# Gate rows fetched pair by pair, the first scores of the third attention moved up, the last gated chunk normalized on VectorE, attention roots by log and exp, in a two-block float32 transformer kernel

## The chip, the core and the metric

The kernel runs on one core of one Trainium2 chip. The metric is the device time of one launch in microseconds (us), the median of several runs. All data are float32 in HBM.

## The reference

One sequence of 256 tokens, width 1024, goes through two blocks. All matrices are float32.

```python
# first block
x = x + 0.5 * swiglu(rmsnorm(x, ff1_norm), w_gate, w_up, w_down)        # width 2816
proj = rmsnorm(x, mix_norm) @ w_in                                      # gMLP a, q, k, v, gate logits
y_a = gmlp_spatial_gating(gelu(a_in), ...)
y_b = stick_breaking_attention(q, k, v)                                 # 16 heads of 64
g_a, g_b = split(sigmoid(g_logits + b_gate))
x = x + (g_a * (y_a @ w_branch_a) + g_b * (y_b @ w_branch_b)) @ w_out
x = x + 0.5 * swiglu(rmsnorm(x, ff2_norm), ...)
x = rmsnorm(x, final_norm)
# second block
x = x + moba_attention(rms_norm(x) @ w_qkv) @ w_o[0]    # 256 tokens: one block, causal, ALiBi
x = x + squared_relu_mlp(rms_norm(x), ...)              # width 4096
k, v, c = shared_kv(x)                                  # c: running sum of log_sigmoid(h @ w_f + b_f)
x = x + forgetting_attention(rms_norm(x) @ w_q, k, v, c) @ w_o[1]
#   logit[t, s] = q.k / 8 + c[t] - c[s], causal, softmax
x = x + squared_relu_mlp(rms_norm(x), ...)
return rms_norm(x, final_norm)
```

## The kernel before, in words

**Precision.** A float32 product is made of three passes with operands split into a high part (a cast, on ScalarE) and a low part (the difference, on VectorE): low by high, high by high, high by low (`three`, L1273). The feed-forward up products put two of these side by side (L1356 and L1363).

**The weight pipeline.** Every weight tile is a *unit*. The SP queue sends unit c into one of four raw slots (`send`, L281) once the low part of unit c - 4 has been taken (`room`, L277). ScalarE casts it (`hi`, L571, the activation is L578), VectorE subtracts (`lo`, L857, the subtraction is L863), TensorE waits for the low part (`ready`, L1270) and multiplies (L1276 for everything but the up products). The order in which each engine takes units and its other work is written out by hand; an engine never passes over an instruction that waits. The cores of the loops are the same in each stage: `ffn`, `attention`, `chunks`, `w_o`, each once per engine.

**Feed-forward, gated (ff1, ff2).** Eleven chunks of 256 hidden columns. Per chunk TensorE makes four banks of up products, VectorE adds the two halves of each bank (L912, four reductions), POOL multiplies by the token scale `rbc` (`normalized`, L506, instruction L514, in two parts, the first once two reductions are done), ScalarE takes Silu (L622), VectorE multiplies (L919), ScalarE and VectorE split the product (L631, L932), and TensorE runs the down products of the chunk after the up products of the next one. After the last chunk there is no next one. Between chunks of ff1 POOL issues side loads (`side_load`, L425): two layer norm rows of 512 KB at m = 2 and 3, the gate bias broadcast to all partitions into `gates`, 1 MB for each token half, at m = 4 and 6, and a norm row of 512 KB at m = 8.

**Attention (stick, moba, fox).** Units 0 to 7 of a stage are v, for all heads; then four units per pair of heads, two for q and two for k. While v is computed, ScalarE sums the squares of x (`stat`, L580: table set load at L582, Square L589, Sqrt L592), VectorE takes the reciprocal (`root`, L866), ScalarE loads the table set with exp and log again (L703) and goes on with units 6 and 7. In moba two such roots follow each other: the first scales x by the first block's final norm (`final`, L872, instruction L878), the second is taken of the scaled x. Then q and k of pair 0 are projected (`project`, L1424) and copied out with the token scale by VectorE (L978 for q, L983 for k). The scores are L1452 and L1454. VectorE adds the bias and takes the row maximum (`first_part`, L993 and L995), ScalarE takes exp (L658), VectorE normalizes (`second_part`, L1013), TensorE transposes (`middle`, L1474), ScalarE copies (L681), TensorE multiplies by v (`weighted`, L1487 and L1491). A cycle does the middle of pair p, the scores of p + 1, the projection of p + 2.

**Before that loop** the three stages differed in one place. Stick and moba: project pair 0, scores of pair 0, project pair 1. Fox: project pair 0, project pair 1, wait for the gate sums, scores of pair 0; on VectorE q and k of pair 1 are copied out before `first_part(0)`.

**Fox only.** The log forget gates are summed over tokens on TensorE (`gate_sums`, L1516 to L1524, placed before unit 7). VectorE copies the sums (L1058, L1059) and only then takes units 8 and on. POOL writes the sums to DRAM (L555) and reads them back broadcast to all partitions into `c_all`, 16 heads of 128 KB each, in four transfers of 2, 4, 4 and 6 heads issued one behind the other (L559, grouping at L49). `biases` (L445) makes the bias of a pair of heads from it (L460, L462, L467); it waits for the group that holds the head. Biases of pairs 0 and 1 come first, then POOL copies v for the pair (L480, which waits for the weighted product of two pairs back) and the biases of the next pair.

Of the kernel before, what the change touches and what calls it, by code (L numbers as in the profile page):

```python
# [48 lines left out]
C_GROUPS = ((0, 2), (2, 4), (6, 4), (10, 6))  # L49
# [4 lines left out]
STAT = {"ms_done": 2, "rms_done": 2, "rstd_done": 2}  # L54

# [11 lines left out]
def att_sems(extra):  # L67
# [11 lines left out]
    ("turn_mix", TR(1)), ("stat_mix", STAT), ("stick", att_sems(STICK)),  # L79
# [4 lines left out]
    ("turn_moba", TR(1)), ("stat_final1", {**STAT, "x_done": 2}),  # L84
    ("stat_moba", STAT), ("moba", att_sems(SOFT)),
    ("w_o0", {"units": 8, "x_done": 4}),
    ("turn_mlp0", TR(1)), ("stat_mlp0", STAT), ("mlp0", mlp_sems(N_MLP)),
    ("turn_fox", TR(2)), ("stat_fox", STAT), ("fox", att_sems(SOFT)),
# [52 lines left out]
def two_blocks(nc, x_in, ff1_norm, ff1_w_gate, ff1_w_up, ff1_w_down, mix_norm, w_in, b_gate, gmlp_ln_g,  # L141
# [4 lines left out]
    with ctx:  # L146
# [3 lines left out]
        def sem(name):  # L150
# [89 lines left out]
            "c_ready", "ct_done", "cn_done", "ct_out", "c_in0", "c_in1", "c_in2", "c_in3", "shift_done", "stored")}  # L240
# [164 lines left out]
        def _(pool):  # L405
# [19 lines left out]
            def side_load(m):  # L425
# [14 lines left out]
            def causal(buf, h):  # L440
                v = buf[:, h, 0:512].rearrange("p (b t) -> p b t", b=2)[:, :, 0:P]
                return pool.affine_select(out=v, in_=v, compare_op=ALU.is_gt, fill=0.0, base=0,
                                          pattern=[[0, 2], [1, P]], channel_multiplier=-1)

            def biases(phase, pr):  # L445
# [3 lines left out]
                for h in range(2):  # L449
# [5 lines left out]
                    else:  # L455

                        for g, (first, _) in enumerate(C_GROUPS):
                            if n == first:
                                pool.wait_ge(s[f"c_in{g}"], 16)
# [9 lines left out]
                        ins.then_inc(s["bias_done"], 1)  # L469

# [35 lines left out]
            def normalized(phase, n, between=lambda m: None):  # L506
# [3 lines left out]
                for m in range(n):  # L510
# [53 lines left out]
        def _(act):  # L564
# [15 lines left out]
            def stat(phase, ready=None):  # L580

                act.preload_act_table_set("sqrt_and_others")  # L582
                for tok in range(TOK):
# [3 lines left out]
                    elif tok == 0:  # L587
# [5 lines left out]
                        .then_inc(s["rms_done"], 1)  # L593

# [45 lines left out]
            def attention(phase, soft, turn_b, stats):  # L640
# [56 lines left out]

                hi(b + 4)
# [4 lines left out]
                act.preload_act_table_set("natural_log_exp_and_others")  # L703
# [87 lines left out]
            attention("stick", False, lambda: turned("turn_mix", 1, [(xt_hi, 1)]), lambda: stat("stat_mix"))  # L791
# [25 lines left out]
            def two_stats():  # L817
                stat("stat_final1")

                stat("stat_moba")  # L820
# [10 lines left out]
            attention("fox", True, lambda: turned("turn_fox", 1, fox_sets), lambda: stat("stat_fox"))  # L831
# [24 lines left out]
        def _(dve):  # L856
# [14 lines left out]

            def final(phase):  # L872

                for tok in range(TOK):
# [3 lines left out]
                    dve.scalar_tensor_tensor(x[:, tok, :], x[:, tok, :], rstd_f[:, tok:tok + 1], row_gain[:],  # L878
                                             ALU.mult, ALU.mult).then_inc(s["x_done"], 1)
# [18 lines left out]
            def ffn(phase, n, stats):  # L898
# [3 lines left out]
                def chunk(c, m, before=lambda: None):  # L902
# [4 lines left out]
                    for q in range(4):  # L907
                        if q < 3:
                            dve.wait_ge(s["up_done"], at(phase, "up_done") + 3 * m + q + 1)
                        else:  # L910
# [3 lines left out]
                            .then_inc(s["g_done"], 1)  # L914
                    lo(c + 7)
# [55 lines left out]
            def attention(phase, kind, turn_b, stats):  # L971
# [179 lines left out]
            def first_stats():  # L1151
# [17 lines left out]
                      lambda: root("stat_mix"))  # L1169
# [17 lines left out]
            dve.wait_ge(s["gate_in"], 32)  # L1187
# [496 lines left out]
```

## Time and profile before

| What | Value |
|---|---|
| median of 3 runs | 1290.17 us (1289.05 to 1290.55) |
| the profiled execution, own time | 1290.61 us |
| its span, first to last instruction | 1288.8 us |
| TensorE (PE) busy | 1240.5 us, 96% |
| VectorE (DVE) busy | 821.1 us, 64% |
| ScalarE (ACT) busy | 642.1 us, 50% |
| GpSimd (POOL) busy | 177.3 us, 14% |
| mean granted TensorE clock | 0.989 of full |
| DMA | 221.77 MB, mean 172 GB/s |

PE is TensorE's matmuls, PEld its weight loads. Times in a timeline or a chain are in us from the start of the span. Square brackets behind a row give how long the engine had been idle before it and what ended that. The granted clock is a share of full speed: 1.00 is 2.4 GHz, 0.50 is 1.2 GHz. An execution takes 1.8 us more than its span.

### The profile page before, as it was taken

The numbers are of one execution on the slowest core, as the hardware profiler recorded it, in microseconds if no ns is written. First come the engines' busy times: TensorE is split into PE (matmuls) and PEld (weight loads), VectorE is DVE, ScalarE is ACT, GpSimd is POOL, SyncE is SP. The second block draws the span as 40 slices with busy tenths as digits, with TensorE's granted clock in tenths as the row PEclk, the third lists the DMA queues.
The fourth block names the chain that finished last, engine by engine and source line by source line (L and its number), as shares of the span: only waits on it lengthen the run. The fifth ranks groups of instructions, "written<-read, shape, count | busy, mean of one in ns | idle before, by whom it ended". The sixth has DMA issues, their size and how long they took to land.

```text
span 1288.8 us, 17749 instructions
## 1 busy us (share of the span) xinstructions
PE 1240.5 (96%) x6854; PEld 1057.0 (82%) x6854; DVE 821.1 (64%) x1276; ACT 642.1 (50%) x1016; POOL 177.3 (14%) x229
## 2 busy tenths in 40 slices
PE   6999999999999999999999999999999699999997
PEld 5788887898878878888878878888888587888886
DVE  4666676454676566666666767866663476785753
ACT  5444446565654445444456656544445365654442
POOL 0222220022030002222202310000000451000000
PEclk9999999999999999999999999999998799999999
DMA  6676654444746454656654445765542444576550
GB/s 192 209 235 213 195 190 148 131 115 131 241 148 199 163 164 149 195 191 201 193 170 135 128 151 191 262 197 184 194 130 56 153 133 164 185 255 195 187 176 33
DMA packets 174973, 221.77 MB, mean 172 GB/s; under 512 B 9708, under 2 KB 104536, under 8 KB 174632
## 3 DMA queue, kind: packets, MB, share of 16 engines
q1 hardware_dynamic: 173112, 213.20, 52.1%
q0 software_dynamic: 1472, 6.38, 1.5%
q8 instruction: 54, 0.88, 0.3%
q10 hardware_dynamic: 304, 1.05, 0.2%
q14 instruction: 31, 0.25, 0.1%
HBM read 219.53 MB, written 1.06 MB: 171 GB/s over the span
## 4 chain that ended last, share of the span: by engine, by line
PE 74%; DVE 10%; DMA 6%; ACT 4%; POOL 3%; issue 1%; SPq 1%; ACTq 0%; DVEq 0%; POOLq 0%
PE bank L1276 46%; PE bank L1356 14%; PE bank L1363 7%; DVE w_lo L863 5%; DMA raw<-in_ff_w_up 4%; POOL work L514 3%; ACT w_hi L578 2%; DVE work L912 1%; PE bank L1487 1%; DMA raw<-in_w_kv 1%; PE bank L1299 1%; PE bank L1474 1%; DVE xt L894 1%; ACT xt L604 1%; DVE work L919 1%
## 5 line engine op out<-in xcount | busy, mean ns | idle before, releaser
L863 DVE TENSOR_TENSOR w_lo<-raw,w_hi 128x512 fp32r<-128x512 f32 (+1 forms) x496 | 510.7, 1048 | 249.0 <-ACT w_hi L578 247.0
L578 ACT ACTIVATE w_hi<-raw 128x512 fp32r<-128x512 f32 (+1 forms) x496 | 432.3, 898 | 289.9 <-DMA raw<-in_ff_w_up 91.9
L1356 PE MATMUL bank<-xt,w_hi 128*128 128x512 f32 x1216 | 320.3, 396 | 3.5 <-DVE work L912 2.3
L1356 PEld LDWEIGHTS bank<-xt,w_hi 128*128 128x128 f32 x1216 | 215.4, 190 | 42.9 <-DVE work L912 3.8
L1363 PEld LDWEIGHTS bank<-xt,w_lo 128*128 128x128 f32 x1216 | 171.0, 190 | 15.4
L1363 PE MATMUL bank<-xt,w_lo 128*128 128x256 f32 x1216 | 175.4, 282 | 0.0
L1276 PE MATMUL bank<-w_hi,xt 128*128 128x512 f32 x512 | 161.1, 396 | 3.0 <-DVE w_lo L863 2.1
L1276 PE MATMUL bank<-w_hi,yt_lo 128*128 128x512 f32 x336 | 131.9, 393 | 2.0 <-DVE yt_lo L1018 2.0
L1276 PE MATMUL bank<-w_hi,yt_hi 128*128 128x512 f32 x336 | 130.9, 390 | 0.0
L1276 PE MATMUL bank<-w_lo,yt_hi 128*128 128x512 f32 x336 | 130.9, 390 | 0.0
L1276 PE MATMUL bank<-xt,w_hi 128*128 128x256 f32 x640 | 118.5, 286 | 0.0
L1276 PEld LDWEIGHTS bank<-w_hi,xt 128*128 128x128 f32 x512 | 95.7, 190 | 26.1 <-issue 3.9
L514 POOL TENSOR_TENSOR work<-work,rbc 128x512 f32<-128x512 f32 x44 | 76.7, 1763 | 285.0 <-DVE work L912 285.0
L1276 PEld LDWEIGHTS bank<-xt,w_hi 128*128 128x128 f32 x640 | 101.3, 195 | 0.0
L1276 PE MATMUL bank<-xt,w_lo 128*128 128x256 f32 x320 | 95.1, 297 | 5.6 <-DVE kt L983 5.6
L1276 PE MATMUL bank<-w_lo,xt 128*128 128x512 f32 x256 | 100.5, 393 | 0.0
L912 DVE TENSOR_REDUCE work<-bank 128x256 f32<-128x512 f32 x152 | 94.2, 682 | 0.0
L1276 PE MATMUL bank<-w_hi,ht_lo 128*128 128x512 f32 x224 | 88.2, 394 | 3.8 <-DVE ht_lo L932 3.8
L1276 PE MATMUL bank<-w_hi,ht_hi 128*128 128x512 f32 x224 | 88.0, 393 | 0.0
L1276 PE MATMUL bank<-w_lo,ht_hi 128*128 128x512 f32 x224 | 87.8, 392 | 0.0
L1276 PEld LDWEIGHTS bank<-w_hi,yt_lo 128*128 128x128 f32 x336 | 63.1, 188 | 15.7 <-issue 2.8
L1276 PEld LDWEIGHTS bank<-w_lo,yt_hi 128*128 128x128 f32 x336 | 63.1, 188 | 13.2
(181 smaller groups left out, 1216.3 us busy)
## 6 DMA issues: line engine op xcount, KB each, us to landing
raw<-in_w_up SPq DMA_DIRECT2D x64, 512.0 KB, 4.3
raw<-in_w_down SPq DMA_DIRECT2D x64, 512.0 KB, 4.2
raw<-in_ff_w_gate SPq DMA_DIRECT2D x88, 256.0 KB, 4.3
raw<-in_ff_w_up SPq DMA_DIRECT2D x88, 256.0 KB, 4.9
raw<-in_ff_w_down SPq DMA_DIRECT2D x88, 256.0 KB, 2.7
raw<-in_w_in SPq DMA_DIRECT2D x40, 512.0 KB, 4.6
raw<-in_w_in SPq DMA_DIRECT2D x32, 256.0 KB, 3.0
raw<-in_moba_w_qkv SPq DMA_DIRECT2D x32, 256.0 KB, 2.9
```

The costliest lines, as they stand in the source:

```text
L514: pool.tensor_tensor(work[1][:, part, :].rearrange("p (a b) -> p a b", a=2), work[0][:, part, :].rearrange("p (a b) -> p a b", a=2), by_token,
L578: act.activation(w_hi[:, c % RING, 0:w], raw[:, c % RAW, 0:w], ACT.Copy).then_inc(s["hi_ready"], 1)
L604: act.activation(dst[:, k, :], src, ACT.Copy, scale=scale).then_inc(s["tr_hi"], 1)
L863: dve.tensor_tensor(w_lo[:, c % RING, 0:w], raw[:, c % RAW, 0:w], w_hi[:, c % RING, 0:w].bitcast(F32), ALU.subtract).then_inc(s["lo_ready" ...
L894: dve.scalar_tensor_tensor(low[:, k, :], src, gain[:, 8 * g + k:8 * g + k + 1], high[:, k, :].bitcast(F32), ALU.mult, ALU.subtract)\
L912: dve.tensor_reduce(work[0][:, q // 2, (q % 2) * S:(q % 2 + 1) * S], up_banks(m)[q][:].rearrange("p (a b) -> p b a", a=2), AX_X, ALU.add)\
L919: dve.tensor_tensor(work[2][:, 1, :], work[2][:, 0, :], work[1][:, 1, :], ALU.mult)\
L1276: ins = pe.matmul(dst, p, q, start=first and n == 0, stop=last and n == 2)
L1299: ins = pe.transpose(banks[b][:, o:o + P], src[:, tok, k * P:(k + 1) * P], ident[:])
L1356: ins = pe.matmul(up_banks(m)[q][:], w_h[:, k % 2, q * P:(q + 1) * P], flat(xt[:, k, :, :]), start=k == 0, stop=False, skip_group_check=True)
L1363: ins = pe.matmul(up_banks(m)[q][:, 0:S], w_l[:, k % 2, q * P:(q + 1) * P], xt_hi[:, k, :], start=False, stop=k == KT - 1, skip_group_chec ...
L1474: ins = pe.transpose(t_bank[h][:, o * P:(o + 1) * P], work[1][:, h, o * P:(o + 1) * P], ident[:])
```

## The change

1. **Fox, rows of the gate sums.** The four transfers become eight, one per pair (256 KB). Pairs 0 and 1 are issued where the four were; that of pair p + 2 behind the biases of pair p. A bias waits for its own pair's transfer.
2. **Fox, order.** TensorE and VectorE take the order of the two other attentions: the scores of pair 0 before the projection of pair 1, `first_part(0)` before the copies of pair 1. The wait for `cn_done` on TensorE goes.
3. **ff1 and ff2, last chunk.** VectorE multiplies by the token scale itself, behind the second and the fourth reduction, each time after a wait for its own reduction.
4. **Attention roots.** ScalarE takes both sums of squares, then one Ln and one Exp with scale -0.5 over both token columns; Sqrt, VectorE's reciprocals and the load of the Sqrt table set go, and the set with exp and log is loaded ahead of unit 4's cast instead of ahead of unit 6's.
5. **ff1, gate bias.** Four transfers of 512 KB at m = 4, 5, 6 and 7 instead of two of 1 MB.
6. **branch_a.** VectorE takes unit 7's low part behind the first evacuation instead of ahead of it.

```diff
-C_GROUPS = ((0, 2), (2, 4), (6, 4), (10, 6))
+ROOT = {"ms_done": 2, "rms_done": 1, "rstd_done": 1}
...
-                if m in (4, 6):
-                    tok = m // 2 - 2
-                    pool.dma_start(gates[:, tok, :], b_gate.broadcast_to([P, 2 * D])).then_inc(s["gate_in"], 16)
+                if 4 <= m < 8:
+                    tok, half = divmod(m - 4, 2)
+                    pool.dma_start(gates[:, tok, half * D:(half + 1) * D],
+                                   b_gate[:, half * D:(half + 1) * D].broadcast_to([P, D])).then_inc(s["gate_in"], 16)
...
+            def gate_row(pr):
+                rows = c_dram[2 * pr:2 * pr + 2, :].rearrange("(a h) t -> a h t", a=1)
+                pool.dma_start(c_all[:, 2 * pr:2 * pr + 2, :], rows.broadcast_to([P, 2, S]))\
+                    .then_inc(s[f"c_in{pr % 2}"], 16)
...
-                        for g, (first, _) in enumerate(C_GROUPS):
-                            if n == first:
-                                pool.wait_ge(s[f"c_in{g}"], 16)
+                        if h == 0:
+                            pool.wait_ge(s[f"c_in{pr % 2}"], 16 * (pr // 2 + 1))
...
+                if phase == "fox" and pr + 2 < PAIRS:
+                    gate_row(pr + 2)
...
-                for m in range(n):
+                for m in range(n - 1):
                     between(m)
...
-            for g, (h, n) in enumerate(C_GROUPS):
-                rows = c_dram[h:h + n, :].rearrange("(a h) t -> a h t", a=1)
-                pool.dma_start(c_all[:, h:h + n, :], rows.broadcast_to([P, n, S])).then_inc(s[f"c_in{g}"], 16)
+            gate_row(0)
+            gate_row(1)
             pairs("fox")
...
+            def inverse_root(phase, dst=rstd):
+                act.wait_ge(s["x_done"], at(phase, "x_done"))
+                for tok in range(TOK):
+                    act.activation(work[2][:].rearrange("p a b -> p (a b)"), x[:, tok, :], ACT.Square,
+                                   scale=1.0 / 32.0, accum_out=ms[:, tok:tok + 1]).then_inc(s["ms_done"], 1)
+                    act.wait_ge(s["ms_done"], at(phase, "ms_done") + tok + 1)
+                act.activation(rms[:], ms[:], ACT.Ln, bias=eps[:]).then_inc(s["rms_done"], 1)
+                act.wait_ge(s["rms_done"], at(phase, "rms_done") + 1)
+                act.activation(dst[:], rms[:], ACT.Exp, scale=-0.5).then_inc(s["rstd_done"], 1)
...
+                act.preload_act_table_set("natural_log_exp_and_others")
                 hi(b + 4)
                 turn_b()
                 hi(b + 5)
                 stats()
                 act.wait_ge(s["rstd_done"], at(phase, "rstd_done"))
-                act.preload_act_table_set("natural_log_exp_and_others")
                 hi(b + 6)
...
+                        if gated and m == n - 1 and q % 2:
+                            dve.wait_ge(s["g_done"], at(phase, "g_done") + 4 * m + q + 1)
+                            dve.tensor_tensor(work[1][:, q // 2, :].rearrange("p (a b) -> p a b", a=2),
+                                              work[0][:, q // 2, :].rearrange("p (a b) -> p a b", a=2),
+                                              rbc[:].unsqueeze(1).broadcast_to([P, 2, S]), ALU.mult)\
+                                .then_inc(s["nrm_done"], 1)
                     lo(c + 7)
...
                 k_evac(b + 8, 0, 0)
-                if kind == "fox":
-                    q_evac(b + 12, 0, 1)
-                    k_evac(b + 12, 0, 1)
                 first_part(0)
                 lo(b + 16)
                 second_part(0)
-                if kind != "fox":
-                    q_evac(b + 12, 0, 1)
-                    lo(b + 17)
-                    k_evac(b + 12, 0, 1)
-                else:
-                    lo(b + 17)
+                q_evac(b + 12, 0, 1)
+                lo(b + 17)
+                k_evac(b + 12, 0, 1)
...
-            for u in range(4, 8):
+            for u in (4, 5, 6):
                 lo(b + u)
             evac_a(0, 0, b + 3, 0)
-            for u in (8, 9):
+            for u in (7, 8, 9):
                 lo(b + u)
...
             def two_roots():
                 dve.wait_ge(s["gain_in2"], 16)
-                final("stat_final1")
-                root("stat_moba")
+                dve.wait_ge(s["rstd_done"], at("stat_moba", "rstd_done"))
+                for tok in range(TOK):
+                    scaled(tok)
                 dve.wait_ge(s["rstd_done"], at("moba", "rstd_done"))
                 dve.tensor_tensor(rstd[:], rstd[:], rstd_f[:], ALU.mult).then_inc(s["rprod_done"], 1)
...
                 for n in range(4):
                     project(b + 8, 0, n)
-                if kind == "fox":
-                    pe.wait_ge(s["qt_done"], at(phase, "qt_done") + 1)
-                    for n in range(4):
-                        if n == 2:
-                            pe.wait_ge(s["kt_done"], at(phase, "kt_done") + 1)
-                        project(b + 12, 0, n)
-                    pe.wait_ge(s["cn_done"], 1)
-                    scores(0, 0)
-                else:
-                    scores(0, 0)
-                    for n in range(4):
-                        project(b + 12, 0, n)
+                scores(0, 0)
+                for n in range(4):
+                    project(b + 12, 0, n)
```

`scaled(tok)` is the instruction of L878 by itself. In the stages stick, moba and fox `stat` and `root` are replaced by `inverse_root` and nothing; the feed-forward stages and the last norm keep `stat` and `root`.

## Rows read from the trace of the kernel before

**Rows 1.** Timeline of VectorE, branch_a: start, length, instruction, idle before and releaser.

```profile
439.65 0.69 DVE L1121 TENSOR_TENSOR work<-bank,gates 128x512 f32<-128x512 f32 x1 [4.79 <-PE bank L1276]
```

**Rows 2.** Timeline of TensorE, fox, pair 1's first projection to pair 0's weighted product.

```profile
1001.63 0.29 PE L1276 MATMUL bank<-xq_hi,w_lo 128*128 128x256 f32 x1
...
1010.11 0.58 PE L1276 MATMUL bank<-xt,w_lo 128*128 128x256 f32 x1 [5.58 <-DVE kt L983]
...
1021.55 1.66 PE L1474 MATMUL bank<-ident,work 128*128 128x128 f32 x6 [4.97 <-DVE work L1013]
...
1028.29 0.65 PE L1487 MATMUL bank<-work,vn 128*64 128x256 f32 x4
```

**Rows 3.** Chain that ended last, 955 to 1085: start, length, what.

```profile
996.01 12.33 DMA raw<-in_w_kv
```

**Rows 4.** DMA issues, whole run: tile, queue, count, KB each, median us to landing.

```profile
raw<-in_w_kv SPq DMA_DIRECT2D x16, 256.0 KB, 3.0
gates<-in_b_gate POOLq DMA_DIRECT2D x2, 1024.0 KB, 6.0
...
row_gain<-in_final_norm POOLq DMA_DIRECT2D x2, 512.0 KB, 4.8
...
c_all<-c_dram POOLq DMA_DIRECT2D x1, 768.0 KB, 10.9
...
c_all<-c_dram POOLq DMA_DIRECT2D x1, 256.0 KB, 6.5
```

**Rows 5.** Timeline of POOL, fox: first biases, and v's copy in a cycle.

```profile
1002.30 0.40 POOL L460 TENSOR_TENSOR bias<-cn,c_all 128x128 f32<-128x128 f32 x1 [4.47 <-DMA c_all<-c_dram]
...
1004.04 0.40 POOL L460 TENSOR_TENSOR bias<-cn,c_all 128x128 f32<-128x128 f32 x1
...
1046.10 0.52 POOL L480 COPY vn<-side 128x256 f32<-128x256 f32 x1 [3.62 <-PE bank L1491]
```

**Rows 6.** Windows, fox: length, busy by engine, PE clock, DMA share, GB/s.

```profile
1000.00:1005.00 5.00, 4.53 (x39) 4.33 (x38) 0.19 (x1) 0.63 (x1) 2.56 (x6) 1.00 1.03 364
...
1010.00:1015.00 5.00, 4.89 (x23) 4.89 (x24) 0.39 (x2) 0.00 (x0) 0.67 (x2) 0.50 0.18 52
```

**Rows 7.** Timeline of TensorE, moba: the same stretch, in the order of moba.

```profile
696.65 0.49 PE L1452 MATMUL bank<-kt,qt 64*128 64x128 f32 x4 [0.61 <-DVE kt L983]
...
708.06 0.65 PE L1487 MATMUL bank<-work,vn 128*64 128x256 f32 x4
```

**Rows 8.** Timeline of ScalarE and TensorE, moba, behind the roots.

```profile
680.44 1.28 ACT L703 ACT_TABLE_LOAD   x1 [0.22 <-DVE rstd L870]
...
684.11 0.73 PE L1276 MATMUL bank<-w_hi,xt 128*128 128x512 f32 x2 [1.05 <-DVE w_lo L863]
```

**Rows 9.** Timeline of VectorE, last chunk of ff1.

```profile
194.51 2.48 DVE L912 TENSOR_REDUCE work<-bank 128x256 f32<-128x512 f32 x4
...
198.97 0.69 DVE L919 TENSOR_TENSOR work<-work 128x512 f32<-128x512 f32 x1 [1.26 <-POOL work L514]
```

**Rows 10.** Timeline and chain of TensorE, last down products of ff1 and of ff2.

```profile
202.68 0.47 PE L1276 MATMUL bank<-w_hi,ht_lo 128*128 128x512 f32 x1 [2.46 <-DVE ht_lo L932]
...
202.68 5.96 PE bank L1276 x18
...
658.53 0.47 PE L1276 MATMUL bank<-w_hi,ht_lo 128*128 128x512 f32 x1 [1.32 <-DVE ht_lo L932]
...
658.53 4.36 PE bank L1276 x18
```

**Rows 11.** Windows of ff1, POOL chunk to POOL chunk, around the side loads.

```profile
65.19:81.88 16.69, 16.69 (x90) 14.36 (x89) 11.04 (x15) 7.61 (x10) 4.06 (x3) 1.00 0.69 221
...
115.26:133.65 18.39, 17.64 (x94) 14.73 (x92) 11.05 (x15) 7.60 (x10) 4.08 (x4) 1.00 0.68 228
149.80:166.94 17.14, 17.14 (x92) 14.79 (x91) 11.04 (x15) 7.61 (x10) 4.08 (x3) 1.00 0.67 213
```

More of the change, by code:

```diff
@@ L78 @@
     ("turn_ff1", TR(1)), ("stat_ff1", STAT), ("ff1", ff_sems(N_FF)),
-    ("turn_mix", TR(1)), ("stat_mix", STAT), ("stick", att_sems(STICK)),
+    ("turn_mix", TR(1)), ("stat_mix", ROOT), ("stick", att_sems(STICK)),
     ("a_in", {**PROJ_SEMS(4), "units": 16}), ("gates", {**PROJ_SEMS(4), "units": 16}),
@@ L83 @@
     ("turn_ff2", TR(1)), ("stat_ff2", STAT), ("ff2", ff_sems(N_FF)),
-    ("turn_moba", TR(1)), ("stat_final1", {**STAT, "x_done": 2}),
-    ("stat_moba", STAT), ("moba", att_sems(SOFT)),
+    ("turn_moba", TR(1)), ("stat_final1", {**ROOT, "x_done": 2}),
+    ("stat_moba", ROOT), ("moba", att_sems(SOFT)),
     ("w_o0", {"units": 8, "x_done": 4}),
     ("turn_mlp0", TR(1)), ("stat_mlp0", STAT), ("mlp0", mlp_sems(N_MLP)),
-    ("turn_fox", TR(2)), ("stat_fox", STAT), ("fox", att_sems(SOFT)),
+    ("turn_fox", TR(2)), ("stat_fox", ROOT), ("fox", att_sems(SOFT)),
     ("w_o1", {"units": 8, "x_done": 4}),
@@ L239, in two_blocks @@
             "wf_hi_done", "wf_lo_done", "f_ready", "fz_done", "fabs_done", "fexp_done", "fln_done", "logf_done",
-            "c_ready", "ct_done", "cn_done", "ct_out", "c_in0", "c_in1", "c_in2", "c_in3", "shift_done", "stored")}
+            "c_ready", "ct_done", "cn_done", "ct_out", "c_in0", "c_in1", "shift_done", "stored")}
         def tiles(w):
@@ L790, in _ @@
             turned("turn_mix", 0, [(xt_hi, 1)])
-            attention("stick", False, lambda: turned("turn_mix", 1, [(xt_hi, 1)]), lambda: stat("stat_mix"))
+            attention("stick", False, lambda: turned("turn_mix", 1, [(xt_hi, 1)]),
+                      lambda: inverse_root("stat_mix"))
             chunks("a_in", gelu)
@@ L817, in two_stats @@
             def two_stats():
-                stat("stat_final1")
-                stat("stat_moba")
+                inverse_root("stat_final1", rstd_f)
+                inverse_root("stat_moba")
             attention("moba", True, lambda: turned("turn_moba", 1, [(xt_hi, 10)]), two_stats)
@@ L830, in _ @@
             act.activation(wf_hi[:], wf[:], ACT.Copy).then_inc(s["wf_hi_done"], 1)
-            attention("fox", True, lambda: turned("turn_fox", 1, fox_sets), lambda: stat("stat_fox"))
+            attention("fox", True, lambda: turned("turn_fox", 1, fox_sets),
+                      lambda: inverse_root("stat_fox"))
             w_o("w_o1", [(xt_hi, 6)], "turn_mlp1")
@@ L870, in root, with scaled @@
                     dve.reciprocal(dst[:, tok:tok + 1], rms[:, tok:tok + 1]).then_inc(s["rstd_done"], 1)
+            def scaled(tok):
+                dve.scalar_tensor_tensor(x[:, tok, :], x[:, tok, :], rstd_f[:, tok:tok + 1], row_gain[:],
+                                         ALU.mult, ALU.mult).then_inc(s["x_done"], 1)
             def final(phase):
@@ L1168, in _ @@
             attention("stick", "stick", lambda: turned("turn_mix", 1, [(xt_lo, xt_hi, 1)]),
-                      lambda: root("stat_mix"))
+                      lambda: None)
             chunks("a_in")
@@ L1186, in _ @@
                     .then_inc(s["ln_done2"], 1)
-            dve.wait_ge(s["gate_in"], 32)
+            dve.wait_ge(s["gate_in"], 64)
             chunks("gates", gate_bias)
@@ L1242, in two_roots @@
                 dve.wait_ge(s["gain_in2"], 16)
-                final("stat_final1")
-                root("stat_moba")
+                dve.wait_ge(s["rstd_done"], at("stat_moba", "rstd_done"))
+                for tok in range(TOK):
+                    scaled(tok)
                 dve.wait_ge(s["rstd_done"], at("moba", "rstd_done"))
@@ L1257, in _ @@
             dve.tensor_tensor(wf_lo[:], wf[:], wf_hi[:].bitcast(F32), ALU.subtract).then_inc(s["wf_lo_done"], 1)
-            attention("fox", "fox", lambda: turned("turn_fox", 1, fox_sets), lambda: root("stat_fox"))
+            attention("fox", "fox", lambda: turned("turn_fox", 1, fox_sets), lambda: None)
             w_o("w_o1", lambda: turned("turn_mlp1", 0, [(xt_lo, xt_hi, 6)]))
```

2 lines of the change are left out of this document (removed).

## The prediction

> **What bounds the kernel now.** I read the shares first: TensorE is busy for 96% of the span (the table above), so an edit can only pay where TensorE stands still, runs at the lower clock, or will do so. Next came the view of waits for TensorE, then the chain at each of its waits, then the timelines there. Three places matter.
>
> In fox TensorE stands still twice on the way into the loop: 5.58 us ahead of pair 1's k projection, for VectorE's copy of k of pair 0, and 4.97 us ahead of the first transposes [rows 2]. The chain leads from the first wait to the transfer of one weight tile, which took 12.33 us and landed at 1008.34 [rows 3]; the same kind of transfer takes 3.0 us in the median [rows 4]. While it was under way the DMA engines were full, at 364 GB/s [rows 6]: the four transfers of gate rows were in flight, 2 MB, the longest for 10.9 us [rows 4]. After the stop the granted clock was 0.50, which is 1.2 GHz [rows 6].
>
> In moba TensorE waits 1.05 us for the low part of unit 6, which is late since ScalarE first does the roots and a table load of 1.28 us [rows 8]. At the ends of ff1 and ff2 it waits 2.46 and 1.32 us for the last chunk's hidden values [rows 10]. The same 18 down matmuls then take 5.96 us in ff1 and 4.36 in ff2 [rows 10]: the longer stop is followed by the lower clock, 1.60 us dear.
>
> **Fox, order and rows.** The stretch from the start of pair 1's projection (TensorE done with pair 0) to pair 0's weighted product is 1028.29 - 1001.63 = 26.66 us [rows 2]. Moba has the new order and the same work: its scores start at 696.65 after a wait of 0.61, so TensorE was done with pair 0 at 696.04, and the weighted product starts at 708.06, 12.02 us later [rows 7]. If fox does what moba does it gains 26.66 - 12.02 = 14.64 us. The second wait goes because bias, exp and normalization run beside the projection of pair 1.
>
> The new order makes k of pair 0 urgent: it needs units 10 and 11 of the stage multiplied, and on VectorE units 14 and 15 stand ahead of it. Unit 15 is the transfer of rows 3. It was issued at 996.01; TensorE went on at 1010.11, 1.77 us after it landed [rows 2, 3]. What will its landing be? With no rows, not before 996.01 + 3.0 = 999.0 [rows 3, 4], and by throughput four units sent together are 1 MB, which at 364 GB/s take 2.9 us [rows 6] behind a start-up of some two; I say 1000.1. With rows, 0.5 MB instead of 2 MB competes. At 364 GB/s that is 1.4 us; by proportion, 2 MB having cost 1008.3 - 1000.1 = 8.2, it is 2.1. I take 1.4, as the row measures the engines full, and get 1001.5. TensorE then starts the scores at 1001.5 + 1.77 = 1003.3, a wait of 1.6 instead of moba's 0.61, 1.0 lost of 14.64: **13.6 us**. The bounds are 14.6 (landed by 1000.5) and 12.9.
>
> The Trainium skill ("DMA: Bandwidth & Descriptors", Where 436 GB/s comes from) puts about 358 GB/s on HBM reads of one core and 436 on the fabric. The trace agrees with the first, at 364. By the second the rows would cost 1.2 us and the gain in fox would be 13.8.
>
> The biases have to come in time too. Pair 0's rows landed at 1002.30 amid 2 MB (6.5 us, so issued at 995.8) [rows 4, 5]; with only 0.5 MB of rows I expect about 1001. A head's bias takes 1.74 us [rows 5], so both are there at 1004.5, when the scores are ready at 1004.2. That is hidden, since the projection of pair 1 lasts beyond 1010. The rows of later pairs are issued two pairs ahead: about 13 us before they are wanted, against 6.5 to 10.9 in the worst burst [rows 4]. The issue costs POOL about half a microsecond per pair, and POOL idles 3.62 us ahead of v's copy in a cycle [rows 5]: nothing. Weights queued behind are cast later than they land by more than the extra microsecond. I put the loop at 0, with 1 us against.
>
> **Last gated chunk.** VectorE's four reductions start at 194.51 and last 2.48; then the low part of one unit; then it idles 1.26 us for POOL; L919 starts at 198.97 [rows 9]. Now it does two multiplications of the size of L919, 0.69 each, with about 0.05 for the wait on its own result: 194.51 + 2.48 + 2 x 0.74 = 198.47, and the unit, as wide as L919, less what neighbours overlap, brings it to about 199.0. The work that fills VectorE's idle time is as long as the idle time. What is late next is VectorE itself. I take **0**, between +0.3 and -0.4 (should each wait on its own result cost more), for ff1 and ff2 together.
>
> **Roots.** In stick and fox TensorE has no wait in v's products, so a root that is early gives 0 there; the earlier table load sits where ScalarE waits for transposes. In moba the first sum of squares starts 1.28 earlier, but VectorE's scaling of x then does both tokens after the common root instead of one beside the other, which takes nearly all of it back. Behind the second root no table load stands: 1.28 saved [rows 8]. This covers the whole wait of 1.05 [rows 8]: **1.05 us**, with 0.8 and 1.3 as bounds. What is next is TensorE.
>
> **Gate bias.** ff1 runs in a loop through POOL, VectorE, a freed raw slot, a transfer and a cast, about as long as TensorE's own work (busy for all of the window of 16.69). Windows with 512 KB of side load are 16.69 and 17.14 long; one with 1 MB is 18.39, and in it TensorE is busy 17.64: the one stop of 0.75 [rows 11]. The four windows in question lie between 81.88 and 149.80, 67.92 us [rows 11]. With four at the mean of 16.69 and 17.14, 16.92, it would be 67.7; at 16.69, 66.8. I take the removal of the stop, which lies between 0.2 and 1.1: **0.7 us**. The wait at the end of ff1 stays near 2.46 and its low clock stays.
>
> The Trainium skill ("DMA: Bandwidth & Descriptors", Measured) advises transfers of 1 MiB and more, and its fit has 2.0 us of fixed cost in each. By that two more transfers would cost up to 4 us here if none of it were hidden. The rows have 4.8 us for 512 KB and 6.0 for 1 MB [rows 4], thus a fixed part of 3.6, but it counts only where a weight tile queues behind it.
>
> **branch_a.** VectorE idles 4.79 us ahead of the evacuation [rows 1], so moving a subtraction of 1.2 us behind it frees nothing; unit 7 is still in time. 0.
>
> **Sum.** 13.6 + 0 + 1.05 + 0.7 = 15.35. The profiled execution took 1290.61, so it would be 1275.3; the median of the runs lies 0.4 below it: **1274.8 us**.
>
> **Rivals.**
>
> *The clock drops after the longer wait.* In ff1 a stop of 2.46 us was followed by the low clock, in ff2 one of 1.32 was not [rows 10]; fox's new wait is 1.6 by my sum, 2.4 at the late end. For: it lies between the two, and small score matmuls follow. Price: 1.6, plus 0.8 of the wait: 1277.2. Chance 0.2.
>
> *The end of ff1 loses its clock drop.* If the loop of ff1 gains 1.1, TensorE's last wait shrinks towards ff2's 1.32 and the 1.6 us go as well [rows 10, 11]: 0.4 + 1.6 + some of the wait more, 1272.3. Chance 0.15.
>
> *The split costs.* If each of the four windows takes 17.14 [rows 11], they sum to 68.56, which is 0.64 slower instead of 0.7 faster: 1276.1. This is the page's advice on large transfers as a mechanism of this loop. Chance 0.12.
>
> *The weight tile is late by itself.* If the 12.33 us come from the units sent together and not from the rows, the wait of 5.58 stays, with half speed behind it. The new order alone: scores at 1010.11, weighted product 708.06 - 696.65 = 11.41 later, at 1021.5, plus about 2.6 for 24 matmuls at the lower clock, is 4.2 gained, so 5.9 in all: 1284.3. Against: 3.0 us in the median for the same kind of tile [rows 4]. Chance 0.05.
>
> *Slower: rows come too late in the loop.* A pair's rows are issued only two pairs ahead. From about 13 us of landing time on, POOL, then `first_part`, then TensorE wait, once in each of the three rounds of two pairs. To lose more than 15.4 us the landing has to reach 13 + 5.1 = 18 us; at 19.5, three times 6.5 lost is 1294. Against: 10.9 is the longest, for 768 KB [rows 4]. Chance 0.03.
>
> *It doesn't do what it says*: in fox the projection of pair 1 is already hidden by nothing and the scores only trade places with it, as another operand arrives when the copy of k does now, and a table load is put between Square and Ln: 1289. Chance 0.03.
>
> **Numbers.** The forecast keeps 0.42. The first four cases hold 0.89 between 1272.3 and 1277.2; with the bounds of the terms (fox 0.7 further, the chunk 0.4, the loop 1) the range is 1271.0 to 1280.0. A measurement of this kernel tells about 0.2%, 2.6 us, from no change. Faster 0.93, same 0.03, slower 0.04.
>
> **What would show it.** Right: TensorE's waits of 5.58 and 4.97 gone, one of 1 to 2.4 us ahead of L1452, no window at 0.50 between 1000 and 1015; unit 15 landing within 6 us; 1.05 gone in moba and four table loads fewer, those of L582 ahead of the attentions' roots; L919 of the last chunk where it was; one wait of 0.75 gone in ff1. Wrong: a wait on the biases, transposes in fox still waiting for L1013, POOL waiting for `c_all` in the loop, or an L919 that moved by over 0.4.

## The result and the profile after

The changed kernel takes 1279.68 us (median of 4, 1278.82 to 1281.78), beside 1290.29 for the kernel before on the same chip. The medians lie 10.6 us apart. The ratio on record is 0.9921, 95% interval 0.9904 to 0.9937, which is 10.2 us (8.1 to 12.4). The forecast was 1274.8, the range 1271.0 to 1280.0. The profiled execution took 1278.92, 11.69 less than that of before; I had forecast 15.35. The stages name the missing 3.7.

The page of the kernel after, its span and first parts:

```profile
span 1277.2 us, 17745 instructions
...
PE 1237.6 (97%) x6854; PEld 1055.8 (83%) x6854; DVE 823.2 (64%) x1272; ACT 636.6 (50%) x1012; POOL 176.3 (14%) x231
...
PE 76%; DVE 10%; DMA 5%; ACT 3%; POOL 3%; issue 1%; SPq 1%; ACTq 0%; DVEq 0%; POOLq 0%
```

Four instructions fewer on ScalarE and four on VectorE, DMA on the chain 5% instead of 6%. The mean granted clock is 0.992 instead of 0.989.

**Fox.** The timeline of TensorE after, which answers to [rows 2] (columns as there):

```profile
998.79 0.40 PE L1301 MATMUL bank<-xt,w_hi 128*128 128x256 f32 x2
1002.48 0.49 PE L1477 MATMUL bank<-kt,qt 64*128 64x128 f32 x4 [3.29 <-DVE kt L1013]
...
1010.67 0.82 PE L1499 MATMUL bank<-ident,work 128*128 128x128 f32 x6
...
1015.32 0.65 PE L1512 MATMUL bank<-work,vn 128*64 128x256 f32 x4
```

Both old waits are gone; the transposes (L1499) wait for nothing. TensorE ends pair 0's projection at 999.19, and the weighted product begins at 1015.32, 16.13 us later instead of 26.66. That is 10.5 gained. The one new wait is 3.29 us long; I had said 1.6. The chain after says why, which answers to [rows 3]:

```profile
993.41 7.21 DMA raw<-in_w_kv
1000.64 0.64 ACT w_hi L584
...
1001.92 0.43 DVE kt L1013
1002.48 0.49 PE bank L1477 x4
...
1003.41 7.43 PE bank L1301 x48
```

Unit 15 is still on it, 7.21 us from issue to landing: less than the 12.33 of before, but more than the 5.5 of my working. And pair 1's projection of 48 matmuls takes 7.43 us. The windows (columns as in [rows 6]) show its two halves; the third row is a place further on:

```profile
1003.00:1008.00 5.00, 5.00 (x30) 4.67 (x28) 2.67 (x12) 3.91 (x12) 4.68 (x11) 0.66 0.39 125
1008.00:1013.00 5.00, 5.00 (x44) 4.50 (x43) 4.59 (x10) 1.42 (x4) 4.70 (x10) 1.00 0.53 161
1075.00:1079.00 4.00, 3.84 (x10) 3.09 (x11) 3.48 (x5) 3.34 (x4) 0.00 (x0) 0.59 0.27 65
```

Behind the wait the clock went to its lower level, 1.2 GHz: 30 matmuls in the first five microseconds, 44 in the next. The third row is the same in the output product of fox. There the chain of after, then that of before, read:

```profile
1075.16 12.74 PE bank L1301 x48
```

```profile
1088.04 11.16 PE bank L1276 x48
```

1.58 us lost, that nothing in the change explains: TensorE's stops just ahead are 0.73 and 1.03 us after, and 0.73 and 1.02 before.

**Moba.** TensorE's next wait behind its norm, and ScalarE's table load (answering to [rows 7, 8]):

```profile
694.04 0.49 PE L1477 MATMUL bank<-kt,qt 64*128 64x128 f32 x4 [0.61 <-DVE kt L1013]
```

```profile
664.01 1.28 ACT L715 ACT_TABLE_LOAD   x1
```

The wait of 1.05 is gone, and the load sits ahead of a cast that nobody waits for. From the last down products of ff2 (657.30 after, 658.53 before) to these scores it is 36.74 us, before 38.12: 1.38 gained, where I had 1.05 with 1.3 as the bound. The wait cost more than its idle time. The matmul ahead of it started at 682.67 and the one behind it at 684.11, 1.44 us later, where neighbours start 0.23 apart, and the next one came another 0.11 late: 1.3 in all.

**Last gated chunk.** Timeline of VectorE, then of TensorE and its chain, which answer to [rows 9, 10]:

```profile
195.23 1.28 DVE L935 TENSOR_REDUCE work<-bank 128x256 f32<-128x512 f32 x2
196.55 0.69 DVE L941 TENSOR_TENSOR work<-work,rbc 128x512 f32<-128x512 f32 x1
197.16 1.28 DVE L935 TENSOR_REDUCE work<-bank 128x256 f32<-128x512 f32 x2
198.47 0.69 DVE L941 TENSOR_TENSOR work<-work,rbc 128x512 f32<-128x512 f32 x1
199.08 0.69 DVE L882 TENSOR_TENSOR w_lo<-raw,w_hi 128x512 fp32r<-128x512 f32 x1
199.69 0.68 DVE L949 TENSOR_TENSOR work<-work 128x512 f32<-128x512 f32 x1
```

```profile
203.39 0.47 PE L1301 MATMUL bank<-w_hi,ht_lo 128*128 128x512 f32 x1 [2.12 <-DVE ht_lo L962]
...
203.39 4.34 PE bank L1301 x18
```

From the first reduction to the last product it is 4.46 us, and before it was 198.97 - 194.51 = 4.46. VectorE is never idle now and ends no earlier. But the 18 down products take 4.34 us instead of 5.96: here the low clock of before is missing, though the stop ahead of it is 2.12 us, hardly shorter than 2.46. The change isn't what decides this. The variants a1 and a2 below have ff1 as it was before, and their 18 products take 4.34 and 4.32 us, behind stops of 2.60 and 1.32; b1 and d2 have it as changed, and theirs take 5.97 and 5.96, behind stops of 2.05 and 1.90.

**Gate bias.** The same windows of ff1 (columns as in [rows 11]):

```profile
82.43:99.82 17.39, 17.39 (x94) 14.96 (x93) 11.04 (x15) 7.59 (x10) 4.07 (x4) 1.00 0.69 211
...
132.92:150.72 17.80, 17.31 (x91) 14.46 (x90) 11.04 (x15) 7.59 (x10) 4.06 (x3) 1.00 0.65 209
```

The four, of which the first and the last are shown, sum to 68.29, before to 67.92. One stop of 0.49 stands where one of 0.75 stood. Nothing gained.

Put together, by offsets of the same instruction in the two traces: ff1 0.9, up to the end of ff2 another 0.3, moba 1.4, up to fox -0.2, fox's entry 10.5, fox's output product -1.6, the rest 0.3: 11.6.

### The profile page after: what moved, and what is told of

It reads as the page before. It is cut to its first block, busy times and chain, and to the rows that moved or that the text cites. A ratio compares the mean times of both kernels' runs of the same rounds, so it can differ in the third digit from the quotient of the medians.

```text
span 1277.2 us, 17745 instructions
## 1 busy us (share of the span) xinstructions
PE 1237.6 (97%) x6854; PEld 1055.8 (83%) x6854; DVE 823.2 (64%) x1272; ACT 636.6 (50%) x1012; POOL 176.3 (14%) x231
## 3 DMA queue, kind: packets, MB, share of 16 engines
q10 hardware_dynamic: 304, 1.05, 0.2%
## 4 chain that ended last, share of the span: by engine, by line
PE 76%; DVE 10%; DMA 5%; ACT 3%; POOL 3%; issue 1%; SPq 1%; ACTq 0%; DVEq 0%; POOLq 0%
PE bank L1301 48%; PE bank L1381 15%; PE bank L1388 8%; DVE w_lo L882 5%; DMA raw<-in_ff_w_up 4%; POOL work L521 3%; ACT w_hi L584 1%; DVE work L935 1%; PE bank L1512 1%; PE bank L1324 1%; DVE xt L917 1%; PE bank L1499 1%; SPq L282 1%; DVE work L949 1%; ACT xt L621 1%
## 5 line engine op out<-in xcount | busy, mean ns | idle before, releaser
L521 POOL TENSOR_TENSOR work<-work,rbc 128x512 f32<-128x512 f32 x40 | 70.6, 1784 | 264.7 <-DVE work L935 264.7
```

What stands on the lines that cost most here:

```text
L521: pool.tensor_tensor(work[1][:, part, :].rearrange("p (a b) -> p a b", a=2), work[0][:, part, :].rearrange("p (a b) -> p a b", a=2), by_token,
```

## The experiments

**The parts alone.** Each on the kernel before, beside 30 runs of it (median 1290.38). The gains in us are worked out from the ratios. The medians lie somewhat further apart: 3.0, 7.6, 2.6 and 0.9 us. The last chunk and branch_a were not run alone.

```diff
# a1_order_only: TensorE and VectorE of fox in the order of the other attentions
# a2_rows_only:
-            for g, (h, n) in enumerate(C_GROUPS): ...
+            gate_row(0); gate_row(1)      # then gate_row(pr + 2) behind the biases of pr
# a3_roots_only: inverse_root and the earlier table load
# a4_split_only: b_gate in four transfers of 512 KB
```

> Of the change only the order in fox (scores of pair 0 ahead of the projection of pair 1); the four transfers of gate rows stay. Theory: both parts are needed. The weight tile of unit 15 still takes about 12 us, so TensorE still stops for 5.6 us, now ahead of the scores; only the stop of 5.0 us ahead of the first transposes goes, and the lower clock follows the stop: 4 to 5 us faster than before. Rival: the order alone brings it, 10 us faster. Second rival: the order without the smaller rows makes the copy of k later still, and it is not faster at all.

Measured: 1287.35 (10 runs), ratio 0.9982 [0.9970, 0.9993]; 2.3 us gained. TensorE and the chain:

```profile
1012.30 0.80 PE L1446 MATMUL bank<-kt,qt 64*128 64x128 f32 x4 [9.51 <-DVE kt L983]
...
997.01 13.18 DMA raw<-in_w_kv
```

The two waits have become one of 9.51, not one of 5.6 as expected. The granted clock is 0.50 from 1008 to 1016. The stretch from pair 0's projection (ended 1002.79) to the weighted product (1025.93) is 23.1 us instead of 26.66. The new order alone is worth little, since it puts the first scores straight behind the late weight tile.

> Of the change only the transfers of gate rows pair by pair; the order in fox stays. Theory: unit 15 takes about 7 us instead of 12.3, the stop of 5.6 us ahead of pair 1's k projection goes and with it the lower clock there; the stop of 5.0 us ahead of the transposes stays. 6 to 8 us faster. Rival: the transfers of later pairs slow the loop, and less than 4 us is left.

Measured: 1282.79 (9 runs), 0.9947 [0.9932, 0.9961]; 6.8 us gained.

```profile
1002.82 0.39 PE L1281 MATMUL bank<-xt,w_lo 128*128 128x256 f32 x1 [1.17 <-DVE kt L988]
1011.80 1.63 PE L1479 MATMUL bank<-ident,work 128*128 128x128 f32 x6 [4.98 <-DVE work L1018]
...
993.14 7.76 DMA raw<-in_w_kv
```

The tile lands in 7.76 us, and the wait of 5.58 shrinks to 1.17; the wait for the normalization stays at 4.98, with the granted clock at 0.50 from 1012 to 1016 behind it. The weighted product starts 20.0 us after pair 0's projection. So the two parts save 3.5 and 6.7 us of this stretch alone and 10.5 together: they don't mask each other. Their ratios, 2.3 and 6.8 us, say the same within the intervals.

> Of the change only the roots by log and exp. Theory: only moba gains, the wait of 1.05 us for unit 6's low part: 1.0 to 1.4 us faster, nothing in stick and fox. Rival: the table load and the reciprocals saved also help stick and fox, 3 us faster.

Measured: 1287.73 (10 runs), 0.9981 [0.9966, 0.9997]; 2.4 us, with an interval from 0.4 to 4.4. In its trace the stretch from ff2's last products (657.95) to moba's first scores (694.72) is 36.77 long, the same 1.4 saved as in the whole. What the median has beyond it isn't resolved.

> Of the change only the gate bias in four transfers of 512 KB. Theory from the trace of the changed kernel: the four windows of ff1 do not get shorter (68.3 us there, 67.9 before), so 0 within 0.5 us, unless the lower clock at the end of ff1 goes by chance, 1.6 us. My forecast had 0.7 faster. Rival: two more fixed costs make it 0.6 to 4 us slower.

Measured: 1289.47 (10 runs), 0.9999 [0.9985, 1.0012]. The split is worth nothing, to within 2 us.

**Who holds the weight tile up.** b3 leaves out the rows' transfers altogether (so the bias lacks the gate term of the key). d2 puts four pairs, 1 MB, into the first burst instead of two.

```diff
# b3_no_rows
-            gate_row(0); gate_row(1)      # and all later ones with their waits
+            pool.memset(c_all[:], 0.0)    # once, behind moba
# d2_four_rows
-            gate_row(0); gate_row(1)
+            for pr in range(4): gate_row(pr)     # then gate_row(pr + 4)
```

> The changed kernel without any transfer of gate rows: c_all is set to zero once by POOL and the biases do not wait, so the gate term of the fox bias that belongs to the key is left out. It measures what the eight transfers still cost. Theory: unit 15 then lands 5 us or less after its issue instead of 7.2 and the stop ahead of the scores is 0.6 to 1.5 us: 2 to 3.5 us faster than the changed kernel. Rival: the four weight transfers sent together take 7 us by themselves, and the time is that of the changed kernel.

> The changed kernel with the rows of four pairs (1 MB) sent together at the start instead of two, the other four later. It measures how the landing time of the weight tile of unit 15 grows with the rows in flight: 3.8 us with none, 7.2 with 0.5 MB, 12.3 with 2 MB. Theory: the rows take a full share of the engines beside the weights until one side is done, so the price per MB falls with the amount: 9 to 10.5 us with 1 MB, a stop of 5 to 6.5 us ahead of the scores and 2 to 4 us slower than the changed kernel. Rival: the price is linear from 0.5 MB on, as my sum had it with 4.1 us per MB: 9.3 less 2, about 7.5, and hardly slower than the changed kernel.

b3: 1271.87 (4 runs), 0.9865 [0.9846, 0.9885]. d2: 1279.34 (4), 0.9908 [0.9891, 0.9925]; beside it the changed kernel had 1280.12 (5), 0.9916 [0.9901, 0.9931], label d1_after_again. So d2 isn't slower, as its rival had it; its tile takes 8.1 us, between the rival's 7.5 and the theory's 9.

> The changed kernel once more, for its time beside its variants on one chip, and for the places where the clock falls. Theory: the time is 0.990 to 0.994 of before, and the short stretches at 1.2 GHz of about 1.6 us each lie in other places than in the first profile (there: 48, 1005, 1077), as they follow stops of 1 to 3 us by chance. Rival: the same places again, so that they belong to this kernel's order of work.

SyncE's issues of units 14 and 15 and TensorE's first scores in b3:

```profile
990.31 0.97 SPq L282 DMA_DIRECT2D raw<-in_w_kv  x2
...
997.29 0.49 PE L1473 MATMUL bank<-kt,qt 64*128 64x128 f32 x4 [0.61 <-DVE kt L1009]
```

and the chain's piece in d1 and in d2:

```profile
990.62 5.94 DMA raw<-in_w_kv
```

```profile
993.64 8.14 DMA raw<-in_w_kv
```

Without rows ScalarE casts units 14 and 15 together from 993.99, so unit 15 was there by 994.8, some 3.8 us after its issue at 990.91, and the stretch up to the weighted product is 12.3 us, 3.9 less than in the changed kernel's profile. The expectation for the whole was 2 to 3.5 us, and the ratios say 7; what lies beyond the stretch isn't shown to come from the rows. The dose curve of that one tile over all traces is then: no rows 3.8 us; 0.5 MB 5.9 (d1), 7.2 (the first profile), 7.3 (c1), 7.4 (b1) and 7.8 (a2); 1 MB 8.1; 2 MB 12.3 (13.2 in a1). Half a megabyte costs 2.1 to 3.9, not 1.4. The windows of the changed kernel, from the issue of the rows to the landing, say where my price was off:

```profile
993.00:995.00 2.00, 2.00 (x19) 2.00 (x18) 0.38 (x1) 1.81 (x4) 1.10 (x2) 1.00 0.97 289
995.00:997.00 2.00, 2.00 (x20) 2.00 (x19) 1.58 (x3) 0.94 (x2) 0.00 (x0) 1.00 0.57 181
997.00:999.00 2.00, 2.00 (x19) 1.98 (x17) 0.14 (x1) 0.00 (x0) 0.16 (x1) 1.00 0.80 255
999.00:1001.00 2.00, 0.18 (x2) 0.00 (x0) 0.64 (x1) 0.98 (x2) 1.85 (x5) 1.00 0.94 282
```

Their mean is 252 GB/s. The 364 of [rows 6] is a mean over five microseconds late in a burst of 2 MB. In windows of 2 us from 996 on that burst moves 272, 176, 298, 404 and 398 GB/s, so the rate holds for its end and not for its start. 0.5 MB at 252 is 2.1 us. I haven't tested why the engines are less than full in the two middle windows, nor why they move less than 364 in the outer two, where they are 0.97 and 0.94 busy.

**Where units 12 to 15 come from.** The low parts of units 8 to 11 free the raw slots for them. VectorE and SyncE of the changed kernel:

```profile
990.34 0.41 DVE L1088 COPY ct<-bank 16x256 f32<-16x256 f32 x1 [11.21 <-PE bank L1549]
...
990.89 2.50 DVE L882 TENSOR_TENSOR w_lo<-raw,w_hi 128x512 fp32r<-128x512 f32 x4
...
991.60 0.97 SPq L282 DMA_DIRECT2D raw<-in_fox_w_q  x2
992.81 0.97 SPq L282 DMA_DIRECT2D raw<-in_w_kv  x2
```

VectorE stands 11.21 us before the copy of the gate sums, with four subtractions that need nothing of them queued behind. So four weight tiles are sent just when the rows are. b1 only takes VectorE's copy of k out from behind the late tile; b2 takes the four subtractions ahead of the wait; c3 is b2 with the four old transfers, 2 MB in one burst; c4 is b2 with fox's old order.

```diff
# b2_low_early (VectorE, fox)
+                    for u in range(8, 12):
+                        lo(b + u)
                     dve.wait_ge(s["c_ready"], 1)
...
-                for u in range(8, 14):
+                for u in range(12 if kind == "fox" else 8, 14):
                     lo(b + u)
# b1_copy_first (VectorE, fox; the changed kernel otherwise)
+                k_evac(b + 8, 0, 0)
                 lo(b + 14)
                 lo(b + 15)
-                k_evac(b + 8, 0, 0)
```

> The changed kernel, but in fox VectorE copies k of pair 0 ahead of the low parts of units 14 and 15. Theory: the wait of 3.3 us ahead of the first scores is the place of those two low parts in VectorE's queue, not the data of the scores; it falls to 0.6 and the lower clock behind it goes, while the low parts are still early enough for pair 1's k: 3 to 4 us faster than the changed kernel (1.1% faster than before). Rival: the wait only moves, to pair 1's k projection, which needs units 14 and 15; with scores and q between, less than 1 us is gained.

Measured: 1279.53 (5 runs), 0.9917 [0.9889, 0.9945], as the changed kernel. TensorE:

```profile
997.59 0.49 PE L1480 MATMUL bank<-kt,qt 64*128 64x128 f32 x4 [0.61 <-DVE kt L1013]
1005.54 0.52 PE L1502 MATMUL bank<-ident,work 128*128 128x128 f32 x3 [1.13 <-DVE work L1043]
...
1008.07 0.80 PE L1480 MATMUL bank<-kt,qt 64*128 64x128 f32 x4 [1.25 <-DVE kt L1013]
```

The scores start at once, and the late tile stops VectorE a little later instead: 2.6 us of waits at new places, a granted clock of 0.50 from 1008 to 1014 behind them, and no gain. The rival expected for b1 came true.

> The changed kernel, but in fox VectorE takes the low parts of units 8 to 11 ahead of its wait for the gate sums (c_ready), where it stood still for 11 us. Theory: the raw slots come free some 9 us earlier, units 12 to 15 land before the rows are sent, and the wait of 3.3 us falls to 0.6 with full clock: 3 to 4 us faster than the changed kernel. Rival: 4 low parts of 0.6 us delay the copies of the gate sums or the low parts of units 6 and 7, and the gain is given back.

Measured: 1273.31 (4 runs), 0.9869 [0.9844, 0.9893]. VectorE, SyncE and TensorE:

```profile
977.53 2.50 DVE L882 TENSOR_TENSOR w_lo<-raw,w_hi 128x512 fp32r<-128x512 f32 x4 [0.33 <-ACT w_hi L584]
...
978.25 0.97 SPq L282 DMA_DIRECT2D raw<-in_fox_w_q  x2
979.45 0.97 SPq L282 DMA_DIRECT2D raw<-in_w_kv  x2
...
996.69 0.49 PE L1479 MATMUL bank<-kt,qt 64*128 64x128 f32 x4 [0.61 <-DVE kt L1013]
1005.28 0.49 PE L1479 MATMUL bank<-kt,qt 64*128 64x128 f32 x4 [1.22 <-DVE kt L1013]
...
1009.08 0.65 PE L1514 MATMUL bank<-work,vn 128*64 128x256 f32 x4
```

Against the copy of the gate sums (at 987.24 here) the tiles are sent 9 us ahead, instead of 1.3 behind, and the stretch from pair 0's projection (ended 996.08) to the weighted product is 13.0 us, close to moba's 12.02. No window around it is below 1.00. By the ratios (0.9869 against 0.9921 and 0.9916) four subtractions in another place bring 6 to 7 us beyond the change, give or take 4 by their intervals, without touching the rows: the fastest kernel here that computes everything. What the traces show at the place is less, and what was expected: 13.0 us against 16.1 in the first profile of the changed kernel and 14.8 in d1, that is 1.8 to 3.1. The two profiled executions, of b2 and of the changed kernel, lie 7.9 us apart; 4.8 of that come from three other places (ff1, the gate products at 977 to 984, fox's output product), where b2's low clock was shorter or missing. In the first two d1 has the same without the edit.

> The changed kernel with the low parts of units 8 to 11 early, and with the four large row transfers of before. Theory: with units 12 to 15 landed before the rows are sent, the size of the row transfers no longer matters for the first scores, but pair 0's bias does (1.7 us a head behind rows that land 6.5 us after issue) and units 16 and 17 are sent beside 2 MB: 0 to 2 us slower than with the rows pair by pair. Rival: the large transfers still cost 6 us and more, as they did before the change.

Measured: 1274.49 (4 runs), 0.9873 [0.9847, 0.9899]. TensorE's first scores:

```profile
1000.47 0.49 PE L1480 MATMUL bank<-kt,qt 64*128 64x128 f32 x4 [0.61 <-DVE kt L1014]
```

With the weights out of the way a burst of 2 MB is harmless to the first scores: they wait 0.61 us and the stretch is 12.4 us. Against b2 the old transfers cost 1.2 us in the median, well within the intervals. So with the new order in place, the place of the four subtractions gives what the rows fetched by pair give, without them.

> The changed kernel with the low parts of units 8 to 11 early and the order in fox of before. Theory: the transfers are out of the way, so what is left is the wait ahead of the transposes that the order leaves open: a stop of 5 us, and the lower clock behind it, 6 to 8 us slower than the same kernel with the new order (1273.3). Rival: with operands early the order does not matter.

Measured: 1279.15 (4 runs), 0.9908 [0.9893, 0.9924].

```profile
1011.55 1.66 PE L1507 MATMUL bank<-ident,work 128*128 128x128 f32 x6 [4.95 <-DVE work L1043]
...
1017.65 0.65 PE L1520 MATMUL bank<-work,vn 128*64 128x256 f32 x4
```

Without the late tile the order decides: the wait for the normalization is back at 4.95, the granted clock is 0.50 at 1012 to 1014 behind it, and the ratio is 0.4% above b2's, 5 us, give or take 4 (the two were measured at different times, each beside the kernel before). The stretch says 4.5: 17.5 us against 13.0. Alone (a1) the same edit was worth 2.3 by the ratio and 3.5 in the stretch.

**The normalization of the last chunk back on POOL**, the changed kernel otherwise.

```diff
# c1_norm_pool
-                for m in range(n - 1):
+                for m in range(n):
                     between(m)
```

> The changed kernel with the last gated chunk normalized on POOL as before. Theory: no difference, within 0.5 us, since L949 comes 4.46 us after the first reduction either way. Rival: the two multiplications on VectorE save what POOL's wait cost, and this kernel is 1 to 2 us slower than the changed one.

Measured: 1278.36 (4 runs), 0.9899 [0.9885, 0.9912], beside 0.9916 [0.9901, 0.9931] with it on VectorE. From the first reduction to the last product it is 192.78 to 197.26, 4.48 us, as expected. The intervals overlap: no gain from this part.

## Why the prediction was right and wrong

**Right.** The direction and the mechanism. In fox the transfer of one weight tile behind the gate rows held TensorE, and both old waits went; the biases were never waited for; the loop with its rows two pairs ahead cost nothing (each row transfer landed in 3.9 us in the median, so the slower case with its 18 us was far off). The last chunk was 0, with VectorE as the next bound, as worked out. branch_a gained nothing: the same instructions ahead of it and behind it are 1.0 us earlier in the trace after. In moba the whole wait went; 1.05 became 1.38, as I had counted only the idle time of the stop and not the broken overlap of the matmuls around it.

**Wrong, the step "I take 1.4, as the row measures the engines full".** 0.5 MB of rows cost the tile 2.1 to 3.9 us, in the profiled execution 3.4. I took a rate from the end of a burst of 2 MB for the start of one of 0.5, against the proportion (2.1) that I had beside it. With the true landing the wait is 3.29 instead of 1.6: 1.7 of the 3.7 missing. Two of my signs failed with this step: the wait is above 2.4, and unit 15 took more than 6 us.

**Wrong, the clock as a rival of 0.2.** With a stop twice as long as forecast the case "the clock drops after the longer wait" was the one that came (my third sign, no low window between 1000 and 1015, failed). The length of the stop was a poor guide in ff1, where I had taken it from: behind 2.60 us the clock held, behind 1.90 it fell. At fox's first scores it fell in every trace with a stop there of 2 us or more (2.07, 3.29, 3.63, 4.34 and 9.51) and not in b2, b3 and c3, which have 0.61 there and at most 1.22 behind it. Its price is in the chain: 7.43 us for the 48 matmuls of pair 1's projection, which take 5.94 in moba, 1.5 lost. The wait's 1.7 and the clock's 1.5 are, within 0.1, the 3.1 by which fox fell short (10.5 of 13.6). The rival's time of 1277.2 missed by 2.5: it had 0.8 of the wait's 1.7, and it kept the 0.7 of the gate bias.

**Wrong, the step "I take the removal of the stop", 0.7 for the gate bias.** It measured 0 (0.9999 alone, +0.37 us in the windows). The stop of 0.75 with 1 MB in flight was a single event; with 512 KB a stop of 0.49 came in the same loop.

**Not foreseen, both ways.** ff1's end lost its low clock (1.6 gained) without the cause of my second rival, since the loop gained nothing, the stop is still 2.12, and a1 and a2 lost it too with ff1 as before. Fox's output product caught one (1.58 lost) behind stops as long as before. In the profiled pair these two cancel. A third low stretch, at 48 to 52 behind a stop of 1.84 us, is in this trace and not in d1, the same kernel.

The sum that should have stood there: fox 10.5, moba 1.4, everything else 0, that is 1278.3 as a median. My view of the chain was right but stopped one step early: I asked what slowed the tile, and not why it was sent so late. b2 shows at the place what this left: another 1.8 to 3.1 us.

**Open.** The change against the sum of its parts (2.3 + 6.8 + 2.4 + 0 = 11.5 against 10.2, all by the ratios) is within the intervals; by the medians it is 14.2 against 10.6, which few runs of a kernel that spreads by 3 to 8 us don't resolve either. Why a given stop is followed by the low clock in one execution and not in the next isn't settled.

## What to carry to other kernels

When a transfer on the chain is slow, look also at why it was issued then: here four subtractions that stood behind a wait they didn't need put four weight tiles into the same moment as a burst of broadcasts. Moving the instruction that frees the slot ahead of that wait did more for the first scores than shrinking the burst, and after it the burst's size made no difference that these runs resolve. Where an edit leads to a shorter stop of TensorE, put the clock behind that stop into the sum as a term and not beside it as a rival.

## What the runs showed of the hardware

**The clock.** The executions of one and the same kernel differ by whole low stretches. The profiled execution of the changed kernel had one at 48 to 52, one of some 7 us at 977 to 984, one at 1004 to 1008 and one at 1075 to 1079. Its repetition d1 ran 4 us ahead by then and had the last two at the same places of the program (1000 to 1003 and 1071 to 1075), the one at 977 for only some 3 us, and the one at 48 not at all. So the rival expected for d1, that the places belong to the kernel's order of work, holds for two of the three that it named. b2 had neither of the last two, and one at 1266 to 1270. A stretch behind a stop costs some 1.6 us (5.96 against 4.36, 12.74 against 11.16).

A stretch from about 976 on is in all 14 traces, and it has no stop ahead of it: in the traces of before and after TensorE is never idle between 969 and 991. What it does first there are the 48 matmuls of 16 columns for the gates. In the trace of before they run from 974 on, three of them in 0.33 us; at 978 the clock falls, and from then on three take 0.64.

Over the five runs of d1 the mean granted clock was 0.995 at 1274.68 us, 0.992 at 1279.14 to 1280.21, and 0.989 at 1283.08; in b2 0.997 at 1270.66 and 0.993 at 1276.60. So most of the spread of a kernel here goes with the clock, though not all (b3 has 0.994 both at 1271.80 and at 1275.41), and a single pair of traces can give or take 3 us by it. Stops of 1.0 us in fox's output product had a drop behind them once and not another time, stops of 2.1 us at the end of ff1 too (2.05 and 2.08 with it in b1 and c3; 2.09 and 2.12 without it in d1 and after).

**A slow tile without full engines.** Between 995 and 997 the DMA engines were 0.57 busy at 181 GB/s, while the tile that everything waited for was in flight. The Trainium skill ("DMA: Bandwidth & Descriptors", Queues, rings and completion order) says that each engine takes a packet in turn from each queue that has work. By that, as an estimate, the rows can delay a tile at most by their own bytes, 1.4 us for 0.5 MB at 364 GB/s. The traces have 2.1 to 3.9, and no run here shows why.
